# Eight dense products of a two-block transformer kernel as seven block products each, with its tables and delta-rule solve rearranged

## The reference

```python
# block 0, T tokens: latent attention, then a gated feed-forward
h = alpha*h + gate * (attention(...) @ w_mla_out)
u = modulate(layer_norm(h), shift, scale)
h = alpha*h + gate * ((silu(u @ w_gate) * (u @ w_up)) @ w_ffn_out)      # D_FF = 2816
# block 1, 512 tokens out: gated delta rule, 16 value heads, chunks of 64 tokens, both directions
q, k, v = silu(short_conv(u @ w_qkv))                                   # q on LAT, k and v on T
S_t = g_t * S_(t-1) + beta_t * k_t (v_t - g_t * S_(t-1)^T k_t)^T        # solved chunk by chunk
h = alpha*h + gate * ((rms_norm(S^T q) * silu(u @ w_gdn_z)) @ w_gdn_out)
# feed-forward 1 on LAT; then attention with qk, z gate and out on T; then an s5
# (diagonal state space) mixer, its glu and its z gate on LAT; a last layer_norm
```

## Time and profile before

| | us |
|---|---|
| three runs | 5020.47, 5027.18, 5028.21 |
| median | 5027.18 |
| the profiled execution's own time | 5031.29 |
| its span in the trace | 5028.8 |
| PE busy | 4424.2 (88%) |
| DVE busy | 1856.6 (37%) |
| GpSimd busy | 1299.0 (26%) |
| ACT busy | 1095.0 (22%) |

### The profile page before, as it was taken

How to read it: one execution, slowest core, us unless ns; L and a number is a source line. 1 busy time by engine, 2 the same in 40 slices (tenths; PEclk the granted TensorE clock), 3 DMA queues, 4 the chain that set the end, 5 groups by cost and what they waited for, 6 DMA issues and landing times. The chain is left out here.

```text
span 5028.8 us, 50281 instructions
## 1 busy us (share of the span) xinstructions
PE 4424.2 (88%) x18452; PEld 2709.6 (54%) x18452; DVE 1856.6 (37%) x3562; ACT 1095.0 (22%) x2335; POOL 1299.0 (26%) x1510
## 2 busy tenths in 40 slices
PE   7889899999898656888989999988899888677998
PEld 4566555555455545775434444556655465563443
DVE  6523555511455672432047502034400209900001
...
GB/s 185 151 1 54 122 193 201 190 139 120 42 50 31 78 151 119 82 86 66 72 131 247 191 69 73 56 32 1 0 50 45 59 182 127 249 218 111 76 74 67
DMA packets 245067, 526.64 MB, mean 105 GB/s; under 512 B 141088, under 2 KB 147744, under 8 KB 215328
## 3 DMA queue, kind: packets, MB, share of 16 engines
...
...
## 5 line engine op out<-in xcount | busy, mean ns | idle before, releaser
L195 PE MATMUL P<-hu,ring 128*128 128x512 f32 (+1 forms) x4672 | 1667.9, 520 | 49.4 <-ACT hu L360 22.5
L195 PEld LDWEIGHTS P<-hu,ring 128*128 128x128 f32 x4672 | 891.7, 191 | 825.3 <-issue 762.6
L195 PE MATMUL P<-area,ring 128*128 128x512 f32 (+1 forms) x3104 | 1162.7, 537 | 54.6 <-PEq L1631 28.5
L195 PEld LDWEIGHTS P<-area,ring 128*128 128x128 f32 x3104 | 593.9, 192 | 622.3 <-issue 600.3
L416 POOL TENSOR_TENSOR fold<-mod,vec 128x16 f32<-128x16 f32 (+1 forms) x5 | 1.0, 209 | 1356.0 <-SPq L395 1114.5
L2364 DVE SCALAR_TENSOR_TENSOR hu<-hu,tmp 128x512 f32 (+3 forms) x48 | 45.1, 939 | 749.8 <-ACT tmp L2358 749.8
L1537 POOL TENSOR_TENSOR area<-area 128x512 f32<-128x512 f32 (+2 forms) x128 | 235.6, 1841 | 10.0
L2358 ACT ACTIVATE tmp<-P,mod 128x512 f32<-128x512 f32 x72 | 41.3, 615 | 821.2 <-PE P L195 821.2
L1931 DVE SCALAR_TENSOR_TENSOR area<-area 128x1024 f32<-128x1024 f32 x98 | 214.6, 2190 | 12.1 <-ACT area L2007 7.8
L1536 POOL TENSOR_TENSOR area<-area 128x512 f32<-128x512 f32 (+2 forms) x128 | 210.7, 1646 | 0.0
L1535 POOL TENSOR_TENSOR area<-area 128x512 f32<-128x512 f32 (+2 forms) x128 | 202.2, 1579 | 27.8 <-DMA area<-in_s_bn 23.3
...
## 6 DMA issues: line engine op xcount, KB each, us to landing
...
```

The lines of the kernel that those rows point to most:

```text
L195: last = nc.tensor.matmul(c.P[:, 2 * s + j, a:b], c.ring[:, slot, (j * kt + k) * 128:(j * kt + k + 1) * 128], x[:, k, a:b], start=k == 0, ...
```

## The change

`dense_seven` takes the place of `dense` in eight calls: `mla_out`, `ffn_in0`, `gdn_kv`, `gdn_z`, `ffn_in1`, `att_qk`, `att_z` and `s5_z` (the short name of the change speaks of nine; the diff has these eight). A group's weights and the tokens are seen as 2 x 2 blocks (two output tiles by two halves of 4 k-tiles; two halves of the tokens, 384 for T and 256 for LAT), and seven products of blocks take the place of eight: 7 x 4 k-tiles x 2 rows = 56 rows of 384 (T) or 256 (LAT) columns. The sums of weights are made by DVE in the ring for each group, the sums of activations (`sums`, t1 to t4) once a stage, and sums of products (`parts`, e1, e5, e7) between ACT and DVE. In a stage with a head the first group stays a plain one.

```diff
+            mm = nc.tensor.matmul
+
+            def product(to, a, b, fresh):
+                for k in range(q):
+                    last = mm(to, col(a, k), b[:, k, :], start=fresh and k == 0, stop=k == q - 1, skip_group_check=True)
+                return last
...
+            def body(g, s, first):
+                slot = (at + s) % 2
+                pe.wait_ge(c.ring_ready[slot], landed(g, s))
+                if not first:
+                    pe.wait_ge(freed, g - 1)
...
+                pe.wait_ge(s_made, g * 4 + (1 - 4 * plain))
+                if opening_group:
+                    pe.wait_ge(t_made, 1)
+                product(bank(s, 0, 1), s1, t1, True).then_inc(five_p, 1)
+                pe.wait_ge(s_made, g * 4 + (2 - 4 * plain))
+                if opening_group:
+                    pe.wait_ge(t_made, 2)
+                product(bank(s, 1, 1), s2, t2, True).then_inc(six_p, 1)
+                pe.wait_ge(s_made, g * 4 + (3 - 4 * plain))
+                if opening_group:
+                    pe.wait_ge(t3_made, 1)
+                product(bank(s, 1, 0), wide(slot, 2), t3, True).then_inc(seven_p, 1)
+                pe.wait_ge(s_made, g * 4 + (4 - 4 * plain))
+                pe.wait_ge(five_k, g + (1 - plain))
+                product(bank(s, 0, 1), s4, b22, False).then_inc(s_used, 1)
+                pe.wait_ge(one_k, g + (1 - plain))
+                product(bank(s, 0, 0), wide(slot, 1), b21, False)
+                pe.wait_ge(seven_k, g + (1 - plain))
+                if opening_group:
+                    pe.wait_ge(t_made, 3)
+                product(bank(s, 1, 0), wide(slot, 3), t4, False).then_inc(c.mm_done, 1)
+            pairs(pe, groups, body)
...
+            def body(g, s, first):
+                if not (first and s == 0):
+                    finish(g - 1, 1 - s, g < 3)
+                if plain and first and s == 0:
+                    return
+                eng.wait_ge(one_p, g + (1 - plain))
+                copy(e1, bank(s, 0, 0)).then_inc(one_k, 1)
+                eng.wait_ge(five_p, g + (1 - plain))
+                copy(e5, bank(s, 0, 1)).then_inc(five_k, 1)
+                eng.wait_ge(seven_p, g + (1 - plain))
+                copy(e7, bank(s, 1, 0)).then_inc(seven_k, 1)
+            for g in range(groups):
+                body(g, g % 2, g < 2)
+            finish(groups - 1, (groups - 1) % 2, groups <= 2)
...
+            def sums_of(g, s, first):
...
+                dve.wait_ge(c.ring_ready[slot], landed(g, s))
+                if not fresh:
+                    dve.wait_ge(s_used, g - plain)
+                if fresh:
...
+                    tt(t1, b12, b11, ALU.subtract).then_inc(t_made, 1)
+                tt(s1, a21, a22, ALU.add).then_inc(s_made, 1)
+                if fresh:
+                    dve.wait_ge(t_made, 1)
...
+                tt(s2, s1, a11, ALU.subtract).then_inc(s_made, 1)
+                tt(a21, a11, a21, ALU.subtract).then_inc(s_made, 1)
+                if fresh:
+                    dve.wait_ge(t_made, 2)
+                    tt(t4, b21, t2, ALU.subtract).then_inc(t_made, 1)
+                dve.wait_ge(s_made, g * 4 + (2 - 4 * plain))
+                tt(s4, a12, s2, ALU.subtract).then_inc(s_made, 1)
...
+                        dve.wait_ge(c.mm_done, at + 1)
...
+            def finish(g, s, first):
+                if not (plain and first and s == 0):
+                    dve.wait_ge(c.mm_done, g + (at + 1))
+                    tt(bank(s, 1, 0), bank(s, 1, 0), e1, ALU.add).then_inc(whole, 1)
+                if vec:
+                    dve.wait_ge(act_done, g + 1)
+                    last = None
+                    for j in range(2):
+                        last = vec(g, j, c.P[:, 2 * s + j, :], c.tmp[:, s, j, :]) or last
...
+            def body(g, s, first):
+                if not (plain and first and s == 0):
+                    sums_of(g, s, first)
+                if not (first and s == 0):
+                    finish(g - 1, 1 - s, g < 3)
+                if mods and g < mods.groups:
+                    mods.products(dve, g)
+                if plain and first and s == 0:
+                    return
+                dve.wait_ge(six_p, g + (1 - plain))
+                dve.wait_ge(one_k, g + (1 - plain))
+                tt(e1, bank(s, 1, 1), e1, ALU.add).then_inc(mixed, 1)
+                dve.wait_ge(five_k, g + (1 - plain))
+                dve.wait_ge(seven_k, g + (1 - plain))
+                tt(e5, e5, e7, ALU.add).then_inc(mixed, 1)
+                dve.wait_ge(mixed, g * 2 + (2 - 2 * plain))
+                tt(bank(s, 1, 1), e1, e5, ALU.add)
+                dve.wait_ge(s_used, g + (1 - plain))
+                tt(bank(s, 0, 1), bank(s, 0, 1), e1, ALU.add)
+            for g in range(groups):
+                body(g, g % 2, g < 2)
```

```diff
-        for e in range(2):
+        for e in range(self.each):
             if not isinstance(g, int) or g:
...
-    residual("mla_out", q_all[:, 5:13, :], 16, (0, 1), BOTH, mods=ModStream(c, "mla_out", 44, 4, fresh=0))
-    head = Head(c, "ln1_0", T, vcol("ln1_g0"), vcol("ln1_b0"), BOTH)
+    residual("mla_out", q_all[:, 5:13, :], 16, (0, 1), BOTH, mods=ModStream(c, "mla_out", 44, 4, fresh=0),
+             sums=sums_at(13 * T, 4, T // 2), parts=parts_at(21 * T, T // 2))
...
+
+    def put_aside(sp):
+        sp.wait_ge(head.settled, 1)
+        sp.dma_start(c.spill, aside).then_inc(spilled, 16)
     feed_forward(0, (0, 1), BOTH, hidden,
-                 (lambda pool: s5_tables(c, pool, KF * T, 0, 8), lambda pool: s5_tables(c, pool, KF * T, 8, 12)),
-                 mods=ModStream(c, "ffn_in0", 52, KF, hold=head.unit), head=head)
+                 (lambda pool: s5_tables(c, pool, KF * T, 0, 3), lambda pool: s5_tables(c, pool, KF * T, 3, 7)),
+                 mods=ModStream(c, "ffn_in0", 52, KF, each=1), head=head,
+                 sums=([sums[0], sums[1], u[:, 0:4, T // 2:T], sums[2]], three),
+                 spill=(put_aside, spilled, lambda sp, back: sp.dma_start(h, c.spill).then_inc(back, 16)))
...
+    def put_aside(sp):
+        sp.wait_ge(head.settled, 1)
+        sp.dma_start(c.spill[:, :, 0:LAT], h[:, :, 0:LAT]).then_inc(spilled, 16)
+        sp.wait_ge(spilled, 16)
+    dense(c, "gdn_q", u, LATS, raw_rows, short_conv, late=silu, head=head, settle=put_aside)
     raw_rows, short_conv, silu = convolved(8, BOTH)
...
+    sums = [flat_h[:, 1536 * n:1536 * n + 1536].rearrange("p (k t) -> p k t", k=4) for n in range(4)]
+    dense_seven(c, "gdn_kv", u, T // 2, raw_rows, sums, parts_at(32 * T + 64, T // 2), short_conv, late=silu)
...
+    act, vec = silu_split(o_gdn, LAT // 2)
+    dense_seven(c, "gdn_z", u, LAT // 2, act, sums_at(0, 4, LAT // 2), parts_at(6 * T, LAT // 2), vec,
+                mods=ModStream(c, "gdn_z", 74, 8, fresh=0), head=Again(c, "gdn_z", modcol(56, 0), modcol(48, 0)))
+    residual("gdn_out", o_gdn, 48 + 16, (0,), LATS, mods=ModStream(c, "gdn_out", 90, 3))
...
-                 mods=ModStream(c, "ffn_in1", 96, KF, fresh=1, hold=head.unit), head=head)
+    feed_forward(1, (0,), LATS, hidden, (None, lambda pool: s5_tables(c, pool, KF * T, 7, 10)),
+                 mods=ModStream(c, "ffn_in1", 96, KF, fresh=1, hold=head.unit), head=head,
+                 sums=([hidden[:, 4 * n:4 * n + 4, LAT:T] for n in range(4)], [hidden[:, 16 + 2 * n:18 + 2 * n, LAT:T] for n in range(3)]))
...
+    dense_seven(c, "att_qk", u, T // 2, copy_split(qk, T // 2), sums_at(24 * T + 16, 4, T // 2),
+                [tmp_flat[:, 384 * n:384 * n + 384] for n in range(3)], mods=ModStream(c, "att_qk", 140, 2, hold=head.unit), head=head)
...
+    dense_seven(c, "att_z", u, T // 2, act, sums_at(27 * T, 4, T // 2), parts_at(35 * T, T // 2), vec,
+                pool=lambda pool: s5_tables(c, pool, 16 * T, 10, 13))
+    residual("att_out", qk, 96 + 16, (2, 3), BOTH, pool=lambda pool: s5_tables(c, pool, 16 * T, 13, 16))
...
+    dense_seven(c, "s5_z", u, LAT // 2, act, sums_at(0, 4, LAT // 2), parts_at(4096, LAT // 2), vec,
+                ready=lambda eng: eng.wait_ge(reloaded, 32))
```

```diff
+    GT = [dvn(x) for x in (cut(ring, 3328, 512), cut(ring, 3840, 512), cut(tmp, 1536, 512))]
+    DB = [dvn(x) for x in (cut(ring, 4352, 512), cut(ring, 4864, 512), cut(tmp, 2048, 512), cut(tmp, 2560, 512))]
+    XC, V5 = (cut(ring, 3328 + 768 * n, 768).rearrange("p (b u n) -> p b u n", b=4, u=6) for n in range(2))
...
-    X5 = c.view(at + 2560, 6, 64)
-    V6 = c.view(at + 2944, 6, 64)
+    X5, V6 = (cut(tmp, 768 * n, 768).rearrange("p (d u n) -> p d u n", d=2, u=6) for n in range(2))
...
+                    for d, to in enumerate((od, ev)):
                         for k in range(6):
-                            last = mm(F0[to, 32 * k:32 * k + 32], six(NTF[of, d])[:, k, to], XC[of, k, :], start=True, stop=True)
+                            last = mm(F0[to, 32 * k:32 * k + 32], six(NTF[:, d])[:, k, to], XC[:, 2 * e + d, k, :], start=True, stop=True)
...
                 act.wait_ge(f5, hh + 1)
```

(11 more changed lines are left out.)

302 lines of the change are left out of this document (232 added, 70 removed).

## The result

| | before | changed |
|---|---|---|
| median of four runs | 5023.8 us | 4836.2 us |
| lowest and highest | 5000.7 to 5028.2 | 4823.2 to 4839.6 |
| the profiled execution's own time | 5031.3 | 4833.2 |
| its span | 5028.8 | 4831.4 |

A forecast was written before the change was run, and what follows sets the result against it. PE's matmul columns were taken to bound every changed stage but gdn_heads. Stage terms summed to -157 us, from the profiled 5031.3 to 4874, so the median to 4870 us, range 4815 to 4935.

The forecast's parts named there:

- The price of a group: In the new stages, time goes by columns: T groups 20.7 to 18.1 us, LAT groups 13.8 to 12.15.
- Rival D: Slower: 630 hand-overs between block products, at 0.25 us each, eat all the gain, 5027 us; chance 0.03.
- the DVE cycle of 19.25 us: In gdn_kv DVE becomes the bound, its cycle above PE's 18.1 us; the stage gains 16.6 us.
- sums and `vec` are 13 us of DVE a group: In gdn_z, with two modulation rows, DVE's 13 us a group exceed PE's 12.15; 4.9 us saved over seven groups.
- the +4 for an opening: In gdn_z the opening waits for conditions and the products ahead of the sums, costing 4 us.
- the term was the end of GpSimd: In att_z three POOL pieces, 55 us each, end last, so nothing is gained: 0, bounds -17 and +14.
- about 15.5 of 18: In ffn_in0, DVE's work per group at doubled prices beside POOL, within PE's 18 us; stage forecast -50.8 us.
- the clock, put at -26: In gdn_heads phase 2, full-height small products keep the clock up; half of a possible 52 us taken.
- the copies, put at +11: In gdn_heads phase 2, added ACT copies chained with PE cost 23 us, half of it beside the scan.
- Rival B: The clock stays up all through phase 2 of gdn_heads: 26 us better, 4844 us; chance 0.15.
- Rival C: Full-height blocks in gdn_heads phase 2 lose their overlap: 38 us worse, 4908 us; chance 0.10.
- Rival A: DVE and POOL pace the new stages gdn_kv, att_z and ffn_in0: some 41 us worse, 4911 us; chance 0.20.

The follow-up runs named there:

- the run with GpSimd: In gdn_kv one of each group's sums of products on GpSimd, against the changed kernel with s5 pieces 4 and 2 and half the added copies on DVE; 4818.6 us, ratio 0.9593.
- XC alone: Changed kernel with only the first small product of phase 2 at 128 partitions, the others 32 and 64 deep as before; 4843.5 us, ratio 0.9646.
- at the old height: Changed kernel with V5 and V6 still copied in four and two pieces, but small products 32 and 64 partitions deep as before; 4859.7 us, ratio 0.9679.

## Why the prediction was right, and where it was off

**The price of a group** held: 384 columns stand between 256 and 512, and groups take 18.06 and 12.09 us where nothing else is late. `mla_out`, `att_qk` and `s5_z` came within 1 us. Only `gdn_kv` was put back; for the other seven stages the length of their groups in the trace is the evidence. **Rival D** falls: of the 630 hand-overs between block products 13 show idle time of over 0.15 us, 11.6 us in all, and each of these ends with an operation of DVE or ACT. In `gdn_z` TensorE is busy 100.8 of 100.9 us across 49 of them.

**gdn_kv: right mechanism, term too large.** The step that failed is the DVE cycle of 19.25 us, "12.2, three product sums 1.65, the fourth 0.5, four weight sums 2.7", and that all twelve groups pay it. It is 18.77. The working laid durations end to end: from start to start the four weight sums take 2.52, the three product sums 1.53 and the convolutions 12.1, and these three are 0.4 of the 0.5 us; over twelve groups the cycle is 6 us of the miss. Another 3 are TensorE's lead: it runs the first groups at its own pace, so the mean is 222.2 / 12 = 18.5. A wait of 1.1 us a group, the sign that had been named, did not show: four waits of 0.4 us did. That DVE's cycle is the pace of the later groups is shown by these waits and by the run with GpSimd, where it became longer and the groups with it.

**gdn_z: two steps failed.** "sums and `vec` are 13 us of DVE a group" is too much: the durations of its operations come to 11.3 us a group, and in the changed kernel DVE works 81.8 us in 100.9 and TensorE never waits. (The terms of the 13 aren't given; DVE's waits for ACT, 6.9 us over seven groups, may have been among them.) And the +4 for an opening that "waits for conditions and the products ahead of the sums" forgot the plain first group: the load, ACT's conditions and the activation sums all lie beside its 16 us, so the first block product starts without a gap. With the head first, TensorE also starts earlier: with conditions first it began 8.2 us later. Apart from that, the terms given, 11.4 less 4.9, 4 and 0.5, make -2.0 and not -0.4.

**att_z: the term was the end of GpSimd, and the size was off.** Three pieces took from 3468 to 3621, 51 us each, not 55. It was right that GpSimd ends last and TensorE idles for it (11.3 us, of which 4.3 are there with two pieces or none too), wrong that nothing is left: -9.5. Moving one piece shows the rest, another 8 us. The bounds given for it, -17 and +14, are -15.6 and +17.4 by its own sum, which changes nothing here.

**gdn_q** was +0.8, not +4. The release was the one foreseen, the size of the transfer's time was off, 11.1 us and not 13.6. The DMA view of the changed kernel:

```profile
spill<-hu SPq DMA_DIRECT2D x1, 2048.0 KB, 11.1
```

**ffn_in0** gave 4.5 less than forecast. Its opening waited 2.2 us for t3 where 3.1 were put, but the first group of block products took 22.1 us in all, 4.1 over, at a lower clock behind the wait. The plain group took 24.5 us where the first group had been 23.0, and three later groups 0.8 to 0.9 more than 18.06, behind waits for DVE or ACT while GpSimd worked: "about 15.5 of 18" was a mean and left no room for that. Between eight runs of the same code the stage takes 411.0 to 414.0 us. **ffn_in1** -42 for -38: the start gave 4.6 and not 5, the end and the opening, put at 0.8, cost 0.2, and four groups that had been 0.1 to 1.3 us late before are on time.

**gdn_heads.** Phase 1 -8.9 for -5, within the bounds; the switch +4.8 for +3.5; phase 2 -17.3 for -15. By the windows the two terms look right as well: the clock, put at -26, took 28.8 us off TensorE's busy time, and the copies, put at +11, stand against 11.5 us more of idle time. The first is borne out, by the clock of fourteen profiles. The second is luck as far as the runs tell: idle time grew by 7.1 us without any copy added (XC alone), did not grow with them at the old height, and shrank by a few microseconds with half of them moved. The prediction had no term for idle time that grows because products get shorter.

**Rival B** (clock up throughout) did not come: 0.91. **Rival C** falls outright: 24 rows of 64 columns take 1.43 us at either height, and rows of 32 columns follow each other at 31 ns, 32 partitions deep or 128. The 50 to 60 ns that the rival went by are the price of 64 columns, not of 64 partitions, and so the rows with which the prediction had compared the page bore on neither. The Trainium skill's page "TensorE: Matmul & The Clock Gate", section "Why this matters for your kernels", says that one matmul of K = 32 takes the time of one of K = 128, and the trace agrees by these 31 ns. The same section of the Trainium skill says that small contractions in distinct row groups run at the same time; no run here can show it, since six neighbours in a row read the same 32 partitions.

**Rival A** came neither in `gdn_kv` nor in `att_z` nor in `ffn_in0` at its price: DVE sets the pace of a few groups in each and costs some 2 to 4 us.
